# Half of the experts' weight loads asked for by ScalarE instead of SyncE

## The reference, cut to what matters

```
aff = softmax(h @ w_router); gate, idx = top_k(aff.T, 32)
xe = h[idx]
hid = silu(xe @ w_gate[e]) * (xe @ w_up[e])
out[idx] += (hid @ w_down[e]) * gate          # then x + g2 * out, rmsnorm
```

## Time and profile before

| | |
|---|---|
| median of 3 runs | 1696.08 us (1694.12 to 1696.78) |
| profiled execution | 1696.44 us, span 1694.1 us |
| TensorE busy | 1547.1 us (91%) |
| VectorE busy | 877.0 us (52%) |
| ScalarE busy | 699.0 us (41%) |
| DMA, one hardware queue | 430.57 MB, 69.3% of 16 engines' span |

### The profile page before, as it was taken

The page is one execution under the profiler, slowest core; times in us unless marked ns, Lnnn a source line. Parts: engine busy times, 40 slices in busy tenths (PEclk is TensorE's granted clock), DMA queues, the critical chain, the costliest instruction groups (busy, mean ns, idle before and its releaser), DMA issues.

```text
span 1694.1 us, 31979 instructions
## 1 busy us (share of the span) xinstructions
PE 1547.1 (91%) x13903; PEld 1318.8 (78%) x13905; DVE 877.0 (52%) x1201; ACT 699.0 (41%) x946; POOL 0.2 (0%) x4
## 2 busy tenths in 40 slices
PE   8999999999999999999999999999998766766665
PEld 7999987999999999889999889897884432333232
DVE  6665798855676566766656567965640000000001
ACT  5444546644454445455444556666431110010001
POOL 0000000000000000000000000000000000000000
PEclk9999999999999999999999999999999998988888
DMA  9855579656566555627565433335779999999998
GB/s 294 269 193 194 162 209 329 223 187 198 197 205 214 195 184 176 219 105 258 190 198 198 157 116 109 116 125 222 259 289 427 429 429 428 431 428 429 430 428 342
DMA packets 184670, 431.61 MB, mean 255 GB/s; under 512 B 8388, under 2 KB 150902, under 8 KB 166421
## 3 DMA queue, kind: packets, MB, share of 16 engines
q1 hardware_dynamic: 184596, 430.57, 69.3%
HBM read 428.62 MB, written 1.93 MB: 254 GB/s over the span
## 4 chain that ended last, share of the span: by engine, by line
PE 71%; DMA 18%; DVE 7%; ACT 2%; issue 1%; SPq 1%; DVEq 0%; ACTq 0%
PE banks L895 15%; PE banks L896 15%; PE banks L897 15%; DMA xn<-in_w_exp_up 7%; DMA ring<-in_w_exp_down 5%; DMA h<-in_w_exp_down 5%; PE banks L1689 2%; PE banks L1373 2%; PE banks L1374 2%; PE banks L1375 2%; PE banks L1683 2%; PE banks L1639 2%; PE banks L1276 1%; PE banks L1358 1%; PE banks L1169 1%; PE banks L1508 1%
## 5 line engine op out<-in xcount | busy, mean ns | idle before, releaser
L2364 DVE TENSOR_TENSOR w_split<-ring,w_split 128x1024 fp32r<-128x1024 f32 x288 | 347.0, 1223 | 218.1 <-ACT w_split L1778 217.9
L895 PE MATMUL banks<-x_split,w_split 128*128 128x256 f32 x1600 | 447.0, 279 | 6.0 <-DVE w_split L2364 3.7
L897 PE MATMUL banks<-x_split,w_split 128*128 128x256 f32 x1600 | 444.0, 277 | 0.0
L896 PE MATMUL banks<-x_split,w_split 128*128 128x256 f32 x1600 | 444.0, 277 | 0.0
L1778 ACT ACTIVATE w_split<-ring 128x1024 fp32r<-128x1024 f32 x287 | 297.4, 1055 | 187.5 <-PE banks L897 181.7
L895 PEld LDWEIGHTS banks<-x_split,w_split 128*128 128x128 f32 x1600 | 302.7, 189 | 7.7 <-issue 4.2
L896 PEld LDWEIGHTS banks<-x_split,w_split 128*128 128x128 f32 x1600 | 302.7, 189 | 0.1
L897 PEld LDWEIGHTS banks<-x_split,w_split 128*128 128x128 f32 x1600 | 302.4, 189 | 0.0
L897 PE MATMUL banks<-hid_split,w_split 128*128 128x256 f32 x704 | 194.3, 276 | 0.0
L895 PE MATMUL banks<-hid_split,w_split 128*128 128x256 f32 x704 | 194.3, 276 | 0.0
L896 PE MATMUL banks<-hid_split,w_split 128*128 128x256 f32 x704 | 194.3, 276 | 0.0
(11 more groups left out here) (518 smaller groups left out, 2308.0 us busy)
## 6 DMA issues: line engine op xcount, KB each, us to landing
ring<-in_ffn_w SPq DMA_DIRECT2D x131, 1024.0 KB, 5.1
arena<-in_w_exp_gate SPq DMA_DIRECT2D x19, 2048.0 KB, 33.5
ring<-in_w_exp_down SPq DMA_DIRECT2D x14, 2048.0 KB, 25.4
arena<-in_w_exp_up SPq DMA_DIRECT2D x13, 2048.0 KB, 40.7
ring<-in_w_mod SPq DMA_DIRECT2D x24, 1024.0 KB, 5.0
ring<-in_w_in SPq DMA_DIRECT2D x21, 1024.0 KB, 5.2
squares<-in_w_exp_down SPq DMA_DIRECT2D x7, 2048.0 KB, 43.9
ring<-in_w_exp_gate SPq DMA_DIRECT2D x7, 2048.0 KB, 29.1
```

Source lines behind the costliest of these rows:

```text
L895: mm(out_, hi, moving(0), start=start, stop=False, **kw)
L896: mm(out_, hi, moving(1), start=False, stop=False, **kw)
L897: return mm(out_, lo, moving(0), start=False, stop=stop, **kw)
L2364: ins = dve.tensor_tensor(half_part(n, o, 1), half_slot(n, o, columns), half_part(n, o, 0).bitcast(F32), ALU.subtract)
```

## The change

Of each expert from number 3 on, the pairs of tiles 0 and 1, 2 and 3 (gate) and 4 and 5 (first half of up) are taken out of SyncE's order. ScalarE asks for them on its own hardware queue, for expert e + 2 just behind its copy of the turned hidden rows of expert e (L2276) and ahead of the gathered rows. Places, sizes, sources and the semaphores that announce a landing stay as they are; `exp_tiles` is only defined earlier, so that both engines can use it.

```
+        BY_SCALAR = [i for i in range(36, LAST_TILE, 2) if i % 12 < 6]
+        LOAD_ORDER = [i for i in LOAD_ORDER if i not in BY_SCALAR]
...
@@ ScalarE, in the loop over experts
                 fn(hid_t.rearrange("p (j i) s -> p i j s", i=4),
                    ps[:, 7, 0:256].rearrange("p (i j s) -> p i j s", i=4, j=2), ACT.Copy).then_inc(sem("hid_t_ready"), 1)
+                for i in BY_SCALAR:
+                    if i // 12 == e + 2:
+                        act.wait_ge(slot_free, N_EXPERTS + tile_before(i + 1) + 1)
+                        act.dma_start(pairs[tile_place(i) // 2], exp_tiles[i % 12 // 2][i // 12]).then_inc(tile_full(i), 16)
                 if e % GROUP == GROUP - 1 and not final:
```

More of the change, by code:

```diff
@@ L579, in build @@
         LOAD_ORDER = list(SINGLE) + [30, 32, 22, 36, 38, 40, 42, 34, 44, 48, 46] + list(range(50, LAST_TILE, 2))
+        BY_SCALAR = [i for i in range(36, LAST_TILE, 2) if i % 12 < 6]
+        LOAD_ORDER = [i for i in LOAD_ORDER if i not in BY_SCALAR]
+        exp_tiles = [w[0].rearrange("e (j p k) c -> j e p (k c)", p=P, k=4)[j]
+                     for w in (w_exp_gate_2, w_exp_up_2, w_exp_down_2) for j in range(2)]
         slot_full = [sem(f"slot_full_{i}") for i in range(SLOTS)]
@@ L810, in branch_load @@
                 cols(FIRST["branch"] + j, (w_branch_a_2, w_branch_b_2)[j // 2][0], 512 * (j % 2), 512, 4)
-            exp_tiles = [w[0].rearrange("e (j p k) c -> j e p (k c)", p=P, k=4)[j]
-                         for w in (w_exp_gate_2, w_exp_up_2, w_exp_down_2) for j in range(2)]
             def tile_load(i):
```

## The result

The changed kernel takes 1698.08 us (median of 20 runs, 1696.13 to 1700.05), the kernel before 1695.74 us (20 runs, 1694.00 to 1696.78). The ratio is 1.0016, interval 1.0010 to 1.0022: 2.7 us slower by the ratio, 2.3 us between the medians. The loss is clear of the noise, and its best value lies under the 0.2% (3.4 us) that the prediction took as the bound of "no change". The forecast was 1698.5 us and "within 0.2%". The profiled execution took 1699.03 us with a span of 1696.9 us.

A forecast was written before the change was run, and what follows sets the result against it. The experts' stage was taken as bound by full DMA engines at 429 GB/s. Span 1694.1 + 2.4 = 1696.5 us, plus 2.34 outside it, less 0.36 for the median: 1698.5 us; range 1695.3 to 1703.5 us.

The forecast's parts named there:

- The bound: Experts' stage, from 1270 us on: DMA engines full at 429 GB/s, so the stage lasts as long as its bytes.
- No cost on SyncE or ScalarE: 39 issues off SyncE buy 0; per expert, three waits and three issues (1.3 us) on ScalarE fit its 4.46 us gap.
- The bound from above: ScalarE's three issues each meet a full queue at 5.38 us: 16.1 us, 11.7 over the gap; taken as 0.
- Even sharing: While both queues hold loads, each gets half the DMA rate, so a pair takes 9.8 us.
- some 11 us: From about expert 5 on, TensorE runs this far behind its old place, at no cost so far.
- The end: Experts 14 and 15: last tile still lands at 1683.9 us, but TensorE may reach it late; +2.4 us taken.
- the dry case: ScalarE's queue empties before expert 14 ends; expert 14 ends at 1672.0 us, L3134 starts at 1687.8 us: +2.7 us.
- The 2.4 us of the sum: Cost taken for the late end of expert 14, added to the span of 1694.1 us.
- The order costs nothing: Rival: shares stay even or expert 14 ends by 1669 us, so no change, 1696.1 us; chance 0.15.
- The cold TensorE: Rival: TensorE at a low clock in expert 15; one cold pair +4.1 us, three +7.0 us (1703.1); chance 0.22.
- The rate: Rivals on DMA rate: 1% lower, +4.2 us, chance 0.06; better, at 433 GB/s 3.9 us off, chance 0.04.
- SyncE's queue was not favoured: Rival: SyncE's queue is favoured, up's first pair of expert 15 lands last at 1685 us; +9 us, 1705; chance 0.05.

The follow-up runs named there:

- last_back: Changed kernel with the last expert's three ScalarE pairs given back to SyncE, 36 of 39 loads left on ScalarE; 1696.20 us, ratio 1.0000 to the kernel before.
- halves: Changed kernel with each of ScalarE's pairs asked for as two loads of one tile, rows of 8 KiB; 1705.15 us, ratio 1.0057 to the kernel before.
- only_last: Kernel before with only the three pairs of expert 15 moved to ScalarE, all others left on SyncE; 1698.20 us, ratio 1.0013.
- short_after: Changed kernel with three quarters of the last expert's gate product left out, loads kept; 1696.28 us, ratio 1.0002 to the kernel before.
- ups_too: Changed kernel with ScalarE also asking for the second up pair, 52 loads in all; 1703.10 us, ratio 1.0045 to the kernel before.
- asked_late: Changed kernel with ScalarE asking for the same 39 loads some 12 us later, behind the next spread matrix; 1700.29 us, ratio 1.0025 to the kernel before.

## Why the prediction was right

**The bound** was read rightly: the stage is as long as its bytes, and the change moves none. About 429 GB/s from slice to slice, the last tile at +405.8 against +405.7.

**No cost on SyncE or ScalarE** held. ScalarE's issues took 0.33 to 0.45 us, it never stood in its queue, and last_back shows 36 such loads at no measurable price. The bound from above, a blocked ScalarE, is real: halves showed 10.36 us for two issues. The prediction's 5.38 us for one was not the longest of the kernel before, though:

```profile
1428.30 6.82 SPq L822 DMA_DIRECT2D squares<-in_w_exp_down  x1
```

Three of those would be 20.5 us. What goes with it is how many loads the queue holds: from 1270 us on, an issue of SyncE in the kernel before took 0.33 to 0.43 us with up to eight loads ahead of it that had not landed, and every one of over 0.45 us, up to 6.82, had nine or ten ahead of it. In the changed kernel no issue found more than five.

**Even sharing** held from pair to pair (9.8 us apart in only_last), but a load that finds ScalarE's queue empty or nearly so takes longer: 13.6 to 15.4 us to its landing. So SyncE's pair of expert 1 was held up less than forecast, expert 1 ended at 1305.19 us (forecast 1307.9) and expert 2 at 1323.01 (1327); expert 5 was later, 1411.08 (1405). From expert 5 to expert 13 each end lies 16 to 23 us behind its place before, not "some 11 us". These errors did not reach the end, where only the order of the last loads counts. The reason given for ScalarE getting ahead, SyncE's loads of half the size in odd experts, also holds: in the changed kernel its pairs asked for at 1543.10 and 1543.51 us landed at 1566.2 and 1573.7 us, 7.5 us apart. The Trainium skill (DMA: Bandwidth & Descriptors, "Queues, rings and completion order") has each engine go round-robin between its queues, packet by packet; the 9.8, 7.5 and 7.4 us agree with such turns. How many rows a packet in the page's sense holds, no run here shows.

**The end** went by the dry case. ScalarE's last pair landed at 1631.37 + 32.4 = 1663.8 us, its queue was dry, SyncE's order decided: the last pair of expert 14 came in at 1669.5 us (forecast 1669.2), expert 14 ended at 1672.05 (1672.0), L3140 started at 1687.82 us (1687.8). only_last and last_back show that the last three loads, and no other part of the change, are the loss; short_after shows that TensorE's pace is its last link. The stage became 2.2 us longer in the profile, against 2.4 forecast, and 2.3 us between the medians.

That the last times agree to a few hundredths is luck. The profiled execution after reached the end of expert 0 0.6 us later than the one before; on the stage's own scale L3140 came at +409.0 where the dry case, with its +2.7 us, had +409.6, and expert 14 ended at +393.3 where it had +393.8. The 2.4 us of the sum was a choice between two cases, 0 and 2.7. And the range of 1695.3 to 1703.5 us is wide against a loss of 2.3: no change at all would have lain inside it too.

**The rivals.** "The order costs nothing" is out: the interval begins at 1.0010. The cold TensorE did not come in expert 15: the scatter took 1.99 us and the gate pair 1.93 us, full speed. It came just ahead of it: the granted clock was 0.69 from 1660 to 1670 us, and the last down pair of expert 14 took 2.42 us, where the same pair took 1.92 us in only_last. That 0.5 us is in the loss of the profiled execution; the prediction had allowed for it ("after 2.0 to 3.6 us"). The rate did not move beyond 428 against 429 GB/s. SyncE's queue was not favoured, but its mechanism, a middle tile landing last, is what ups_too brought about: +7.6 us where +9 was priced. In one more detail the prediction was wrong: it expected waits at the second up pair as well as at down, and they are at down alone.

## What to carry to other kernels

Where the DMA engines are full, as here, a second queue buys no bytes and changes their order; ask not how early a load is requested but how many bytes are still to come when the last step of the compute chain begins. Count back from the last landing: compute needs its own time from the last thing that it waits for (15.8 us here from the end of expert 14), and a load that overtakes early leaves fewer bytes to come at the end, behind which compute could catch up. The 36 loads in the middle cost nothing that the runs can see (last_back), the last three cost 2.3 us; asked_late lost 2 us at the start. So check a new order at the first hand-over, where the store is thin, and at the end.

## What the runs showed of the hardware that was not expected

- Two hardware queues with loads under way share by packet. Rows of 16 KiB beside rows of 16 KiB: a pair every 9.8 us from each queue. Rows of 16 KiB beside rows of 8 KiB: a pair every 7.4 us. Whoever cuts loads finer gives bandwidth to the other queue.
- Rows of 8 KiB for 39 of the pairs brought the rate from 428 (changed) to 425 GB/s (halves), and the end of the bytes 3 us later.
- A load asked for on an empty or nearly empty second queue, beside a busy first one, lands 13.6 to 15.4 us after it was asked for (changed, only_last), where those behind it follow every 9.8 us. Why it takes some 4 us more was not tried.
- A queue with nine or ten loads asked for and not landed can stop its issuer, whether they are of 1 or 2 MiB (128 rows each): up to 6.82 us for one issue on SyncE before, 10.36 us for two on ScalarE in halves, with the work of ScalarE behind them. With up to eight, ScalarE's issues in halves took 0.33 to 0.45 us.
